# Hymba decoder layer on one core: x's first half in two DMAs, identity products in TensorE's two opening waits, and VectorE's first copy of x placed behind the first unit's low parts

## The chip, the cores and the metric

The kernel runs on one NeuronCore of a Trainium2 chip. The metric is the device time of one execution in microseconds (us), lower is better. The kernel before takes 471.38 us, the median of three runs (470.81, 471.38 and 471.77). TensorE (PE) multiplies, VectorE (DVE) and ScalarE (ACT) work on elements, GpSimd (POOL) builds constants, and SyncE (SP) issues nearly all DMAs from one instruction stream.

## The reference

One decoder layer over 256 tokens of width 1024, all in float32:

```
u = rms_norm(h, norm_mix);  z = u @ w_in
y_rwkv = rwkv7_time_mix(z[..., :RWKV_IN], ...)       # 8 heads of 64
y_moba = moba_attention(q, k, v)                     # 8 heads of 64, from z
h = h + concat[y_rwkv, y_moba] @ w_mix_out
h = h + cross_attention(rms_norm(h, norm_xattn), rms_norm(mem, norm_mem), w_xq, w_xkv, w_xo)
h = h + square(relu(rms_norm(h, norm_ffn) @ w_ff1)) @ w_ff2
out = rms_norm(h, norm_final)
```

The change touches only the beginning: x is read and transposed, and the first column block of `w_in` is multiplied.

## The kernel before

**Tiling.** Every weight matrix is read in units of 1 MB (mostly 1024 rows by 256 columns), three of which fit into the ring `raw`. A float32 product is made from two float32r parts: ACT rounds a half unit into `w_hi` (`hi`, line 1114, `hi_done`), DVE subtracts it from the raw values and gets `w_lo` (`lo`, line 1622, `lo_done`), and PE adds three products (high by high, high weight by low operand, low weight by high operand). The operand x is treated in the same way: PE transposes it in quarters of 256 columns into the banks B[0] to B[3] (`load`, line 616), ACT writes `op_hi` times the norm's gain (line 1166), DVE writes `op_lo` (line 1740), and `copies` (line 1748) keeps the transposed x in `hT` for the residual.

**Order.** There is no scheduler: each engine's order is a list of calls written by hand at the end of its function. PE's starts with `params(0)`, four `load(0, q)`, `dense(2)`, `params(1)`, `dense(2)`, `spread(0)`, and then `dense(10)`. `dense(n)` runs the next n quarters of the weight stream. The first four quarters are unit 0 (lines 515, 516 and 521, halves s=0 and s=1), and `spread(0)` (line 627) spreads the inverse norm. The quarter behind it is the first of unit 1 (line 549), which waits for `hi(2)` and `lo(2)`. A float32 product of 128x128 shows as two records of PE, a transpose or a float32r product as one.

**Waits.** PE's `load(0, 0)` and `load(0, 1)` wait for `x_in[0]`, `load(0, 2)` and `load(0, 3)` for `x_in[1]`. ACT's `stats(0)` (line 1179) takes the row sums of x and needs all of it. DVE's `diagonal_of(0)` (line 1754) waits for their root, and `spread(0)` waits for that diagonal.

**DMA issues.** SP issues in this order: `norm_mix`, first half of x, first half of unit 0, second half of x, second half of unit 0, twelve small parameter rows (line 351), then unit 1 (line 343), two LoRA matrices (lines 353 and 354), unit 2 and `mem`. From unit 3 on it waits for `hi_done` and `lo_done` of the unit that held the buffer; unit 3 needs `lo(1)`.

## Time and profile before

| | before |
|---|---|
| median of 3 runs | 471.38 us (470.81 to 471.77) |
| the profiled execution | 470.57 us, span 468.8 us |
| PE busy | 453.8 us (97%) |
| PE weight loads | 410.1 us (87%) |
| DVE busy | 322.0 us (69%) |
| ACT busy | 236.6 us (50%) |
| DMA queue q1 | 72.14 MB, 48.3% of 16 engines |
| mean DMA rate | 156 GB/s |

The span runs from the first to the last instruction of the profile; the profiled execution's own time is 1.77 us more. PE is busy in 97% of the span, so what matters is the few places where it isn't. "Idle before" in a row is the time in which that engine stood still before the instruction, and the name behind the arrow is what ended it.

### The profile page before, as it was taken

What the parts mean: (1) busy time and instruction counts of PE and PEld (TensorE: products, weight loads), DVE (VectorE), ACT (ScalarE), POOL (GpSimd) and SP (SyncE); (2) the same over time, 40 slices, a digit from 0 to 9 for tenths busy, and PEclk for the clock granted to TensorE, in tenths of its full rate; (3) what the DMA queues carried; (4) which work ended last, traced back from release to release, by engine and by line L of the source; (5) the groups of instructions that cost most, each with busy time, mean ns of one, the idle gap of its engine ahead of it and who ended that gap; (6) DMA issues with size and microseconds to landing.
All of it is one profiled execution on the core that took longest, in us unless ns stands there. A gap on an engine that the chain in (4) does not pass through costs nothing.

```text
span 468.8 us, 10481 instructions
## 1 busy us (share of the span) xinstructions
PE 453.8 (97%) x4470; PEld 410.1 (87%) x4470; DVE 322.0 (69%) x487; ACT 236.6 (50%) x373; POOL 35.1 (7%) x51
## 2 busy tenths in 40 slices
PE   4999999989999999999999999999999999999994
PEld 4999999989899879999998898888888888888883
DVE  4688999897485557668766368876555656574746
ACT  5789833252444426436444455545465545454534
POOL 8200000000000000071000001340000000000000
PEclk9999999999999999999999999999999999999998
DMA  7973534606050432462552165655546565756502
GB/s 246 334 226 119 180 95 142 215 5 184 3 194 15 153 119 89 137 225 89 180 181 89 35 189 189 218 181 179 180 147 213 185 197 166 251 185 218 188 2 89
DMA packets 60385, 73.05 MB, mean 156 GB/s; under 512 B 1314, under 2 KB 49524, under 8 KB 60340
## 3 DMA queue, kind: packets, MB, share of 16 engines
q1 hardware_dynamic: 60260, 72.14, 48.3%
q8 instruction: 35, 0.57, 0.5%
q0 software_dynamic: 80, 0.26, 0.1%
q14 instruction: 10, 0.08, 0.0%
HBM read 71.35 MB, written 1.05 MB: 154 GB/s over the span
## 4 chain that ended last, share of the span: by engine, by line
PE 90%; DVE 4%; DMA 1%; SPq 1%; ACT 1%; issue 1%; ACTq 0%; DVEq 0%
PE bank L534 13%; PE bank L549 11%; PE bank L550 10%; PE bank L551 10%; PE bank L566 6%; PE bank L568 6%; PE bank L567 6%; PE bank L536 6%; PE bank L915 2%; DMA raw<-in_w_in 1%; PE bank L502 1%; PE bank L503 1%; PE bank L504 1%; PE bank L939 1%; PE bank L488 1%
## 5 line engine op out<-in xcount | busy, mean ns | idle before, releaser
L1622 DVE TENSOR_TENSOR w_lo<-raw,w_hi 128x1024 fp32r<-128x1024 f32 x130 | 160.2, 1239 | 67.2 <-ACT w_hi L1114 67.1
L1114 ACT ACTIVATE w_hi<-raw 128x1024 fp32r<-128x1024 f32 x130 | 136.8, 1057 | 111.0 <-PE bank L551 51.8
L534 PE MATMUL bank<-op,w_hi 128*128 128x512 f32 x256 | 89.1, 398 | 0.0
L549 PE MATMUL bank<-op,w_hi 128*128 128x256 f32 x288 | 83.7, 291 | 0.2 <-DVE w_lo L1622 0.2
L550 PE MATMUL bank<-op,w_hi 128*128 128x256 f32 x288 | 81.4, 283 | 0.0
L551 PE MATMUL bank<-op,w_lo 128*128 128x256 f32 x288 | 81.4, 283 | 0.0
L536 PE MATMUL bank<-op,w_lo 128*128 128x256 f32 x224 | 62.8, 281 | 0.0
L549 PEld LDWEIGHTS bank<-op,w_hi 128*128 128x128 f32 x288 | 55.1, 191 | 1.3 <-issue 0.9
L550 PEld LDWEIGHTS bank<-op,w_hi 128*128 128x128 f32 x288 | 55.2, 192 | 0.2
L551 PEld LDWEIGHTS bank<-op,w_lo 128*128 128x128 f32 x288 | 55.1, 191 | 0.0
L534 PEld LDWEIGHTS bank<-op,w_hi 128*128 128x128 f32 x256 | 46.4, 188 | 8.9
L566 PE MATMUL bank<-w_hi,op_hi 128*128 128x512 f32 x128 | 50.0, 390 | 0.0
L568 PE MATMUL bank<-w_hi,op_lo 128*128 128x512 f32 x128 | 49.8, 389 | 0.0
L567 PE MATMUL bank<-w_lo,op_hi 128*128 128x512 f32 x128 | 49.8, 389 | 0.0
L536 PEld LDWEIGHTS bank<-op,w_lo 128*128 128x128 f32 x224 | 42.3, 189 | 1.3
L549 PE MATMUL bank<-op_hi,w_hi 128*128 128x256 f32 x128 | 37.9, 296 | 0.7 <-DVE op_lo L2019 0.7
L550 PE MATMUL bank<-op_lo,w_hi 128*128 128x256 f32 x128 | 36.2, 283 | 0.0
L551 PE MATMUL bank<-op_hi,w_lo 128*128 128x256 f32 x128 | 36.1, 282 | 0.0
L1147 ACT ACTIVATE tmp<-bank 128x256 f32<-128x256 f32 x32 | 12.2, 382 | 37.7 <-PE bank L534 37.6
L568 PEld LDWEIGHTS bank<-w_hi,op_lo 128*128 128x128 f32 x128 | 24.0, 188 | 5.1
L567 PEld LDWEIGHTS bank<-w_lo,op_hi 128*128 128x128 f32 x128 | 24.0, 188 | 5.0
L566 PEld LDWEIGHTS bank<-w_hi,op_hi 128*128 128x128 f32 x128 | 24.0, 188 | 4.7
(275 smaller groups left out, 712.6 us busy)
## 6 DMA issues: line engine op xcount, KB each, us to landing
raw<-in_w_ff SPq DMA_DIRECT2D x32, 1024.0 KB, 5.4
raw<-in_w_in SPq DMA_DIRECT2D x12, 1024.0 KB, 5.5
raw<-in_w_xkv SPq DMA_DIRECT2D x8, 1024.0 KB, 5.3
raw<-in_w_mix_out SPq DMA_DIRECT2D x4, 1024.0 KB, 5.0
raw<-in_w_xq SPq DMA_DIRECT2D x4, 1024.0 KB, 5.0
raw<-in_w_xo SPq DMA_DIRECT2D x4, 1024.0 KB, 5.7
xval<-in_x SPq DMA_DIRECT2D x2, 512.0 KB, 4.7
raw<-in_w_in SPq DMA_DIRECT2D x2, 512.0 KB, 5.7
```

Of the source, the lines that this page charges most:

```text
L534: last = mm(b[:, :], wh[:, k, :], op_both[0][:, :, k, :], start=first, stop=final)
L536: mm(b[:, 0:T], wl[:, k, :], op_hi[0][:, k, :], start=False, stop=False)
L549: mm(dst, wh[:, k, :], op_hi[which][:, k, :], start=first, stop=False)
L550: mm(dst, wh[:, k, :], op_lo[which][:, k, :], start=False, stop=False)
L551: last = mm(dst, wl[:, k, :], op_hi[which][:, k, :], start=False, stop=final)
L566: mm(dst[:, :], hi, wh[:, k, :], start=first, stop=False)
L567: mm(dst[:, :], hi, wl[:, k, :], start=False, stop=False)
L568: last = mm(dst[:, :], lo, wh[:, k, :], start=False, stop=final)
L915: last = mm(dst, xqT[:, 2 * h + a, tokens_of(n)], xkey[:, 2 * h + a, :], start=(a == 0), stop=(a == 1))
L1114: op(view(w_hi), r, ACT.Copy).then_inc(hi_done, 1)
L1147: op(tmp[:, n % 2, T * half:T * half + T], half_bank(s)[:, T:2 * T], ACT.Copy).then_inc(act_part, 1)
L1622: tt(view(w_lo), r, view(w_hi).bitcast(f32), ALU.subtract).then_inc(lo_done, 1)
```

## The change

The first half of x (columns 0 to 511) is read by two DMAs of 256 columns with a semaphore each, so there are three semaphores: PE's `load(0, q)` waits for `x_in[min(q, 2)]`, and ACT's `stats(0)` waits for all three. PE gets `rouse(3)` ahead of `load(0, 0)` and `rouse(5)` between `load(0, 1)` and `load(0, 2)`: float32 products of the identity by itself into a bank that `dense` overwrites later. On DVE `copies(0)` goes from its place behind `load(0, 0)` to behind `lo(1)`.

```
-        x_in, mem_in, mix_in = [sem("x_in0"), sem("x_in1")], sem("mem_in"), sem("mix_in")
+        x_in, mem_in, mix_in = [sem(f"x_in{i}") for i in range(3)], sem("mem_in"), sem("mix_in")
...
             for half in range(2):
-                c, k = slice(512 * half, 512 * half + 512), slice(4 * half, 4 * half + 4)
-                sp.dma_start(stage[0][:, :, c], x[:, :, c]).then_inc(x_in[half], 16)
+                k = slice(4 * half, 4 * half + 4)
+                pieces = (slice(512, 1024),) if half else (slice(0, 256), slice(256, 512))
+                for i, c in enumerate(pieces):
+                    sp.dma_start(stage[0][:, :, c], x[:, :, c]).then_inc(x_in[2 * half + i], 16)
                 sp.dma_start(first_to[:, k, :], first[:, k, UNITS[0][3]:UNITS[0][3] + 256]).then_inc(first_in[half], 16)
...
                 if m == 0:
-                    pe.wait_ge(x_in[q // 2], 16)
+                    pe.wait_ge(x_in[min(q, 2)], 16)
...
+            def rouse(n):
+
+                for _ in range(n):
+                    mm(dense_bank[1][:, 0:128], ident[:, :], ident[:, :], start=True, stop=True)
...
             params(0)
+            rouse(3)
             load(0, 0)
             load(0, 1)
+            rouse(5)
             load(0, 2)
             load(0, 3)
...
                 if m == 0:
-                    act.wait_ge(x_in[0], 16)
-                    act.wait_ge(x_in[1], 16)
+                    for landed in x_in:
+                        act.wait_ge(landed, 16)
...
             params(0)
             load(0, 0)
-            copies(0)
             load(0, 1)
             lo(0)
             load(0, 2)
             load(0, 3)
             lo(1)
+            copies(0)
             diagonal_of(0)
```

This is how TensorE's list begins before the change; L616 is a transpose of x, `x_in0` and `x_in1` are its halves, and L515 is the first product of unit 0.

```order
L595 MATMUL bank<-ident,prob 128x8 [waits mix_in,pool_const]
L616 MATMUL bank<-ident,xval 128x128 [waits x_in0]
L616 MATMUL bank<-ident,xval 128x128 x3
L616 MATMUL bank<-ident,xval 128x128 [waits x_in0]
L616 MATMUL bank<-ident,xval 128x128 x3
L616 MATMUL bank<-ident,xval 128x128 [waits x_in1]
L616 MATMUL bank<-ident,xval 128x128 x3
L616 MATMUL bank<-ident,xval 128x128 [waits x_in1]
L616 MATMUL bank<-ident,xval 128x128 x3
L515 MATMUL bank<-op,w_hi 128x256 [waits dve_op,hi_done]
```

The same stretch of TensorE after the change, where L618 is the transpose, L625 the identity product and L517 the first product of unit 0.

```order
L597 MATMUL bank<-ident,prob 128x8 [waits mix_in,pool_const]
L625 MATMUL bank<-ident 128x128 x3
L618 MATMUL bank<-ident,xval 128x128 [waits x_in0]
L618 MATMUL bank<-ident,xval 128x128 x3
L618 MATMUL bank<-ident,xval 128x128 [waits x_in1]
L618 MATMUL bank<-ident,xval 128x128 x3
L625 MATMUL bank<-ident 128x128 x5
L618 MATMUL bank<-ident,xval 128x128 [waits x_in2]
L618 MATMUL bank<-ident,xval 128x128 x3
L618 MATMUL bank<-ident,xval 128x128 [waits x_in2]
L618 MATMUL bank<-ident,xval 128x128 x3
L517 MATMUL bank<-op,w_hi 128x256 [waits dve_op,hi_done]
```

Three products stand ahead of the first transpose and five ahead of the ninth; nothing else on TensorE has moved.

This is how VectorE's list begins before the change; L1740 writes `op_lo`, L1748 is the copy of x, L1622 writes `w_lo`, and L1754 waits for the root of the row sums.

```order
L1740 SCALAR_TENSOR_TENSOR op<-bank,par,op 128x256 [waits act_op,dve_params]
L1740 SCALAR_TENSOR_TENSOR op<-bank,par,op 128x256
L1748 COPY hT<-bank 128x512 [waits act_op] x2
L1740 SCALAR_TENSOR_TENSOR op<-bank,par,op 128x256 [waits act_op,dve_params]
L1740 SCALAR_TENSOR_TENSOR op<-bank,par,op 128x256
L1622 TENSOR_TENSOR w_lo<-raw,w_hi 128x1024 [waits hi_done]
L1740 SCALAR_TENSOR_TENSOR op<-bank,par,op 128x256 [waits act_op,dve_params]
L1740 SCALAR_TENSOR_TENSOR op<-bank,par,op 128x256
L1740 SCALAR_TENSOR_TENSOR op<-bank,par,op 128x256 [waits act_op,dve_params]
L1740 SCALAR_TENSOR_TENSOR op<-bank,par,op 128x256
L1622 TENSOR_TENSOR w_lo<-raw,w_hi 128x1024 [waits hi_done]
L1754 RECIPROCAL row_sum<-row_sum 128x2 [waits act_root]
```

The same stretch of VectorE after the change, with L1749 for `op_lo`, L1757 for the copy, L1631 for `w_lo` and L1763 for the reciprocal.

```order
L1749 SCALAR_TENSOR_TENSOR op<-bank,par,op 128x256 [waits act_op,dve_params]
L1749 SCALAR_TENSOR_TENSOR op<-bank,par,op 128x256
L1749 SCALAR_TENSOR_TENSOR op<-bank,par,op 128x256 [waits act_op,dve_params]
L1749 SCALAR_TENSOR_TENSOR op<-bank,par,op 128x256
L1631 TENSOR_TENSOR w_lo<-raw,w_hi 128x1024 [waits hi_done]
L1749 SCALAR_TENSOR_TENSOR op<-bank,par,op 128x256 [waits act_op,dve_params]
L1749 SCALAR_TENSOR_TENSOR op<-bank,par,op 128x256
L1749 SCALAR_TENSOR_TENSOR op<-bank,par,op 128x256 [waits act_op,dve_params]
L1749 SCALAR_TENSOR_TENSOR op<-bank,par,op 128x256
L1631 TENSOR_TENSOR w_lo<-raw,w_hi 128x1024 [waits hi_done]
L1757 COPY hT<-bank 128x512 [waits act_op] x2
L1763 RECIPROCAL row_sum<-row_sum 128x2 [waits act_root]
```

The two copies now stand between the second `w_lo` and the reciprocal.

## Rows read from the trace of the kernel before

**Rows 1.** The page: busy time, and the engines of the chain that ended last.

```profile
PE 453.8 (97%) x4470; PEld 410.1 (87%) x4470; DVE 322.0 (69%) x487; ACT 236.6 (50%) x373; POOL 35.1 (7%) x51
PE 90%; DVE 4%; DMA 1%; SPq 1%; ACT 1%; issue 1%; ACTq 0%; DVEq 0%
```

**Rows 2.** PE's waits: engine, line, releaser, us in total, times, longest.

```profile
PE bank L616 <- DMA xval<-in_x: 3.6, 2, 2.0
```

**Rows 3.** The chain that ended last, opening: start us, us, what.

```profile
7.84 6.93 DMA raw<-in_w_in
14.80 1.07 ACT w_hi L1114
15.96 1.24 DVE w_lo L1622
```

**Rows 4.** Timeline of PE: start us, us, instruction, idle before and what ended it.

```profile
4.62 1.97 PE L616 MATMUL bank<-ident,xval 128*128 128x128 f32 x8 [1.96 <-DMA xval<-in_x]
8.28 1.97 PE L616 MATMUL bank<-ident,xval 128*128 128x128 f32 x8 [1.69 <-DMA xval<-in_x]
10.26 0.41 PE L516 MATMUL bank<-op,w_hi 128*128 128x256 f32 x1
10.48 0.41 PE L515 MATMUL bank<-op,w_hi 128*128 128x256 f32 x1
...
12.12 0.28 PE L515 MATMUL bank<-op,w_hi 128*128 128x256 f32 x1
12.24 0.28 PE L516 MATMUL bank<-op,w_hi 128*128 128x256 f32 x1
...
16.54 0.61 PE L627 MATMUL bank<-prob,ones 128*128 128x128 f32 x4
17.33 0.36 PE L549 MATMUL bank<-op,w_hi 128*128 128x256 f32 x1 [0.18 <-DVE w_lo L1622]
```

**Rows 5.** Timeline of SP's issues of x's second half and of unit 1.

```profile
2.22 0.51 SPq L332 DMA_DIRECT2D xval<-in_x  x1
...
7.84 0.39 SPq L343 DMA_DIRECT2D raw<-in_w_in  x1
```

**Rows 6.** Landing, issues at 1.26 and 2.77: KB, us.

```profile
xval<-in_x SPq DMA_DIRECT2D x1, 512.0 KB, 3.3
...
raw<-in_w_in SPq DMA_DIRECT2D x1, 512.0 KB, 6.9
```

**Rows 7.** Stretches: us, busy us of PE to POOL, granted clock, DMA share, GB/s.

```profile
2.30:4.60 2.30, 0.24 (x1) 0.18 (x1) 0.17 (x1) 0.00 (x0) 2.10 (x7) 1.00 0.94 305
...
9.80:11.30 1.50, 1.50 (x9) 1.50 (x8) 1.50 (x3) 1.49 (x5) 1.42 (x2) 1.00 1.07 332
...
460.00:468.80 8.80, 2.85 (x13) 2.03 (x11) 4.34 (x10) 3.60 (x10) 0.00 (x0) 0.81 0.32 119
```

**Rows 8.** Timeline of DVE and ACT in the opening.

```profile
7.51 1.28 DVE L1748 COPY hT<-bank 128x512 f32<-128x512 f32 x2
...
9.44 1.69 ACT L1166 ACTIVATE op<-bank,par 128x256 fp32r<-128x256 f32 x4 [1.03 <-PE bank L616]
...
11.02 1.06 ACT L1114 ACTIVATE w_hi<-raw 128x1024 fp32r<-128x1024 f32 x1
...
12.19 1.29 DVE L1622 TENSOR_TENSOR w_lo<-raw,w_hi 128x1024 fp32r<-128x1024 f32 x1
...
14.65 0.17 DVE L1754 RECIPROCAL row_sum<-row_sum 128x2 f32<-128x2 f32 x1 [1.17 <-ACT row_sum L1185]
```

**Rows 9.** Timeline of PE behind its longest later idle time.

```profile
100.99 1.37 PE L751 MATMUL bank<-neu,X 32*32 32x32 f32 x128 [1.08 <-DVE neu L1889]
...
102.74 0.28 PE L502 MATMUL bank<-w_hi,op 128*128 128x256 f32 x1
```

**Rows 10.** Short stretches: us, granted clock, DMA share, GB/s.

```profile
8.50:9.00 0.50, 1.00 0.51 172
9.00:9.50 0.50, 1.00 1.03 172
```

More of the change, by code:

```diff
@@ L215, in build @@
         raw_in, first_in = [sem(f"raw_in{i}") for i in range(NRAW)], [sem(f"first_in{i}") for i in range(2)]
-        x_in, mem_in, mix_in = [sem("x_in0"), sem("x_in1")], sem("mem_in"), sem("mix_in")
+        x_in, mem_in, mix_in = [sem(f"x_in{i}") for i in range(3)], sem("mem_in"), sem("mix_in")
         act_sums, act_root, dve_diag, pe_spread_rms = sem("act_sums"), sem("act_root"), sem("dve_diag"), sem("pe_spread_rms")
@@ L330, in _ @@
             for half in range(2):
-                c, k = slice(512 * half, 512 * half + 512), slice(4 * half, 4 * half + 4)
-                sp.dma_start(stage[0][:, :, c], x[:, :, c]).then_inc(x_in[half], 16)
+                k = slice(4 * half, 4 * half + 4)
+                pieces = (slice(512, 1024),) if half else (slice(0, 256), slice(256, 512))
+                for i, c in enumerate(pieces):
+                    sp.dma_start(stage[0][:, :, c], x[:, :, c]).then_inc(x_in[2 * half + i], 16)
                 sp.dma_start(first_to[:, k, :], first[:, k, UNITS[0][3]:UNITS[0][3] + 256]).then_inc(first_in[half], 16)
@@ L603, in load @@
                 if m == 0:
-                    pe.wait_ge(x_in[q // 2], 16)
+                    pe.wait_ge(x_in[min(q, 2)], 16)
                 elif q == 0:
@@ L618, in load, with rouse @@
                 last.then_inc(pe_load, 1)
+            def rouse(n):
+                for _ in range(n):
+                    mm(dense_bank[1][:, 0:128], ident[:, :], ident[:, :], start=True, stop=True)
             def spread(m):
@@ L943, in _ @@
             params(0)
+            rouse(3)
             load(0, 0)
             load(0, 1)
+            rouse(5)
             load(0, 2)
@@ L1172, in stats @@
                 if m == 0:
-                    act.wait_ge(x_in[0], 16)
-                    act.wait_ge(x_in[1], 16)
+                    for landed in x_in:
+                        act.wait_ge(landed, 16)
                 else:
@@ L2046, in _ @@
             load(0, 0)
-            copies(0)
             load(0, 1)
@@ L2052, in _ @@
             lo(1)
+            copies(0)
             diagonal_of(0)
```

## The prediction, made before the changed kernel was run

> **What bounds the kernel now.** I read the page's busy times first: PE is busy in 97% of the span and carries 90% of the chain that ended last [rows 1]. So a saving counts only where PE stands still or runs slowly, and whatever delays PE's stream is carried to the end. Next I read PE's waits. The longest are two for x, 3.6 us together [rows 2], both in the opening. Then the chain in order of time shows what holds the end, and it isn't x. The chain goes from the issue of unit 1 at 7.84 through its landing 6.93 us later (14.77) to ACT's rounding at 14.80 and DVE's low part at 15.96 [rows 3], and from there to PE's first product of unit 1 at 17.33 [rows 4]. Last comes PE's own timeline [rows 4]: eight transposes at 4.62, 1.69 us of idle, eight at 8.28, then the 48 products of unit 0 without a gap, the two norm products (four records from 16.54, done at 17.15), 0.18 us of idle, and unit 1. So two paths meet at 17.33: the weights' path ends there, and PE's own path ends 0.18 us before. From 17.33 on I treat the program as one block whose length doesn't change, since PE is full.
>
> The clock matters in that stretch. Products of 256 columns start 0.22 us apart at 10.26, and 0.12 us apart at 12.12 [rows 4]: 256 columns are 0.213 us at 1.2 GHz and 0.107 us at 2.4 GHz, so the lower level holds until about 11.3 and the upper one follows. The granted clock of 9.80 to 11.30 reads 1.00 all the same [rows 7]; in the opening that column says nothing, and I go by the distances. Ahead of the rise PE did eight transposes, idled 1.69 us, and did eight transposes and seven products.
>
> **The change part by part.** The sum is made against the profiled execution, 470.57 us, which lies 0.8 us under the median of 471.38.
>
> *x's first half in two DMAs, on PE's side.* The first half lands 3.3 us after its issue at 1.26 [rows 6], so at 4.56. A quarter is 256 KB less; at 305 GB/s [rows 7] that is 0.86 us, so I expect it at 3.7 to 3.9. The second quarter ends with the same bytes as before, at 4.6 to 5.0. Transposes, ACT's `op_hi` and DVE's `op_lo` of the first quarter start 0.6 us earlier at most.
>
> *The products by the identity.* The two norm products made four records in 0.61 us [rows 4], 0.11 to 0.12 us of distance, so a float32 product is two records. At the lower clock a record of 128 columns takes about 0.21 us, which the transposes show (eight in 1.97 us less the pipeline's 0.2 [rows 4]). `rouse(3)` is then 6 x 0.21 = 1.3 us from 2.45, over by 3.9: it fits in the 1.96 us of idle ahead of the first transpose, or costs 0.2 us there. `rouse(5)` is 10 x 0.21 = 2.1 us against 1.69 us of idle, but starts up to 0.6 us sooner, at 5.6 to 6.0, and is over by 7.7 to 8.1, ahead of x's second half at 8.2. Cost 0, at worst 0.3 us, and PE's path can bear that, as shown next.
>
> *What the clock gives back.* If the upper level is reached by 8.3, eight transposes go from 1.7 to 1.0 us and the seven slow products from 0.21 to 0.12 us each (0.7 us). PE's path gets 1.3 us shorter: its work ends near 15.8 and not at 17.15. It isn't held up earlier: ACT's four `op_hi` at 9.44 [rows 8] and then `w_hi` of s=1 at 11.02 move 0.5 us forward with the transposes, and PE needs the latter at about 12.2.
>
> *`copies(0)` behind `lo(1)`.* Two copies, 1.28 us in all at 7.51 [rows 8]. Where they stood they held up `op_lo` of the second quarter and `lo(0)`. Where they go, DVE has 1.17 us of idle ahead of the reciprocal at 14.65, for it waits for ACT's root. `lo(1)` ends at 13.48 at the latest (12.19 + 1.29 [rows 8]); with the copies DVE is there at 14.76, 0.11 us late in the worst case, and in the likely one `lo(1)` is over by 13.0 and nothing is late. Behind it stand the diagonal, four short parameter operations and `lo(2)`, which has 0.20 us of slack. Cost 0, at most 0.1 us.
>
> *The same split, on SP's side.* SP issues one DMA more ahead of unit 1. Rows of such issues last 0.39 and 0.51 us [rows 5]; I take 0.45, so unit 1 is issued at 8.3 and not at 7.84. Does it land later? Between 8.5 and 9.0 the DMA engines are busy in a 0.51 share, and from 9.0 on in 1.03 [rows 10]. So they ran partly dry before unit 1 came, and there a later issue is a later landing. But the second half of unit 0, issued at 2.77, landed only 6.9 us later, at 9.67 [rows 6], so some engines were still at it in that hole, and on those a later issue costs nothing. The bounds are 0 and 0.45 us; I take 0.35, nearer to the hole's side. It lies in the path of rows 3 and is carried in full.
>
> The Trainium skill says in DMA: Bandwidth & Descriptors (Queues, rings and completion order) that each DMA engine takes descriptors in the order of its ring. By that rule alone, with rings never empty, the later issue would cost nothing and the sum would be 470.6; the half-empty window of rows 10 says that some rings were empty, and the measurement decides for a cost.
>
> *The sum.* PE's path is ready at about 15.8, the weights' path at 17.33 + 0.35 = 17.7. PE's gain of 1.3 us turns into a longer wait for `lo(2)`, about 1.9 us where it was 0.18. 470.57 + 0.35 = 470.9 against the profiled execution.
>
> *The measured median.* The other three runs of the kernel before are 0.24, 0.81 and 1.20 us above the profiled one. One cause that the rows allow: the rise of the clock comes at another moment in each. Every microsecond by which it comes later than 11.3 costs PE's path 0.5 us, and only 0.18 us of it is covered. A rise at 13.5 would be 1.1 - 0.18 = 0.9 us. After the change PE's path has 1.9 us to spare, so that cost is gone. The skill's page TensorE: Matmul & The Clock Gate (Part 1) also says that the number of slow matmuls at the start differs from run to run of one kernel; one trace can't show it. I allow 0.1 us for scatter with other causes and predict 471.0 us, 0.08% under the median.
>
> **The rivals.**
>
> *A. The clock is worth something and unit 1 isn't late.* For it: the slowest DMA engine had no hole, and 1 us of scatter waits to be removed. Against it: rows 10. Then the runs gather at the profiled 470.57 or a bit under: 470.57 less the 0.18 us that PE had to spare and some tenths if unit 1's bytes come sooner, 470.1 to 470.6, say 470.4, 0.2% faster.
>
> *B. The weights' path gets longer by more than the issue.* `lo(1)` ends up to 0.6 us sooner, so SP asks for unit 3 sooner, while unit 1 is still under way on busy engines; and x's first half now comes in rows of 1 KB where they were 2 KB. Each could cost unit 1 a few tenths. For it: the share is over 1.0 from 9.0 on [rows 10]. Against it: `w_in`'s rows are 1 KB too, and the rate with them is 332 GB/s in 9.80 to 11.30, no less than x's 305 [rows 7]. 470.57 + 0.45 + 0.6 = 471.6, no change that can be told.
>
> *C. The clock falls back in the longer wait.* This is the one on the slower side. PE now idles near 1.9 us ahead of unit 1. If that throws it to 1.2 GHz, the products of unit 1 start 0.21 us apart for as long as the rise takes again: from the first product at 9.9 it took 1.4 us, from 8.28 3.0 us, so half of 1.4 to 3.0 us is lost, 0.7 to 1.5, in the one block that carries everything to the end. With the later issue that is 471.6 to 472.4, and it counts as slower once the fall costs over 1.4 us. For it: at the end of the span, where PE has finished, the granted clock is 0.81 [rows 7]. Against it: after 1.08 us of idle at 100.99 the products start 0.12 us apart [rows 9], and the unit 0 work would come right ahead of this wait.
>
> *D. The change doesn't wake the clock.* Products by an identity may not count, or the rise comes at 11.3 anyway. Then PE's path is 0.5 us better at most from x's first quarter, still ahead of the weights' path, and the time is again 470.9. It has the forecast's time, and I count it there.
>
> The skill's page on the clock gate (Part 4, PE-mode transpose) says that transposes don't count as work for the clock; the trace agrees in so far as eight of them at 4.62 were followed by eight more at the lower level. If the page is right, only `rouse` and unit 0 count.
>
> **How the numbers follow.** The forecast (with D) has 0.60, with its own range 470.6 to 471.4. A has 0.20, B 0.11, C 0.09. A difference under 0.2% (0.94 us) can't be told from none here, so faster means under 470.44 and slower over 472.32. A lies on that edge: half of it counts as faster, and I add 0.10 for medians of the forecast's kind that scatter downwards, since the baseline's own median may be high by chance. That is 0.20 faster. C gives 0.05 and scatter 0.03 slower, 0.08. The rest is 0.72. The range takes A's better end and most of C's: 470.1 to 472.0.
>
> **What would show it right or wrong.** Right: first transpose at 3.7 to 4.1; records of the identity products at 2.45 and 5.6; the first product of unit 0 at 9.2 to 9.9, and 0.12 us between products from there; the copies at 13 to 14.4; unit 1 issued at 8.3 and landed at 14.8 to 15.3; PE idle for 1 to 2 us ahead of line 549's first product, which starts at 17.4 to 17.9. It would be wrong if that first product came before 17.2 (then something I take as fixed has moved), if products behind it started 0.21 us apart (C), or if it came at its old place and the time changed by over 1 us, for then my block from there to the end isn't rigid.

## The result and the profile after

The changed kernel takes 473.62 us, the median of 6 runs (472.41 to 474.04). The kernel before, run beside it, takes 471.43 us (6 runs, 470.81 to 471.79). The ratio is 1.0046 with a 95% interval of 1.0036 to 1.0056. The change makes the kernel 2.2 us slower, and the forecast of 471.0 us and its range both missed. The profiled execution after took 474.0 us with a span of 472.0 us, 3.4 us above the profiled execution before (470.57 us).

The page of the kernel after: busy time, and the chain that ended last by engine (before: [rows 1]).

```profile
PE 457.8 (97%) x4486; PEld 413.7 (88%) x4486; DVE 322.3 (68%) x487; ACT 236.5 (50%) x373; POOL 35.4 (7%) x51
PE 89%; DVE 4%; SPq 2%; DMA 2%; ACT 1%; issue 1%; ACTq 0%; DVEq 0%
```

PE is busy 4.0 us longer. The rows of the 16 new records (eight float32 products) sum to 3.96 us (1.65 + 2.31, below) and stand where PE idled before, so the busy time says little of the end. The DMA's and SP's shares of the chain have gone from 1% to 2% each, and this is the first pointer to the opening.

PE's waits after: engine, line, releaser, us in total, times, longest (before: [rows 2]).

```profile
...
PE bank L551 <- DVE w_lo L1631: 1.6, 1, 1.6
PE bank L618 <- DMA xval<-in_x: 1.4, 2, 0.8
PE bank L553 <- issue: 0.9, 1, 0.9
```

The waits for x have gone from 3.6 to 1.4 us, and the wait for unit 1's low part has gone from 0.18 to 1.55 us. That exchange was forecast. The wait of 1.08 us at line 751 [rows 9] is gone, and 0.94 us with no releaser stands near 95 us instead.

PE's timeline after: start us, us, instruction, idle before and its releaser (before: [rows 4]; 618 is before's 616, 625 the identity product, 551 to 553 are before's 549 to 551).

```profile
2.64 1.65 PE L625 MATMUL bank<-ident 128*128 128x128 f32 x6
4.16 1.11 PE L618 MATMUL bank<-ident,xval 128*128 128x128 f32 x4
5.95 1.12 PE L618 MATMUL bank<-ident,xval 128*128 128x128 f32 x4 [0.67 <-DMA xval<-in_x]
6.86 2.31 PE L625 MATMUL bank<-ident 128*128 128x128 f32 x10
9.93 1.10 PE L618 MATMUL bank<-ident,xval 128*128 128x128 f32 x8 [0.76 <-DMA xval<-in_x]
...
10.99 0.28 PE L518 MATMUL bank<-op,w_hi 128*128 128x256 f32 x1
...
16.98 0.68 PE L634 MATMUL bank<-prob,ones 128*128 128x128 f32 x4
19.21 0.52 PE L551 MATMUL bank<-op,w_hi 128*128 128x256 f32 x1 [1.55 <-DVE w_lo L1631]
19.53 0.41 PE L552 MATMUL bank<-op,w_hi 128*128 128x256 f32 x1
19.74 0.41 PE L553 MATMUL bank<-op,w_lo 128*128 128x256 f32 x1
...
22.52 0.36 PE L551 MATMUL bank<-op,w_hi 128*128 128x256 f32 x1
22.71 0.28 PE L552 MATMUL bank<-op,w_hi 128*128 128x256 f32 x1
...
96.02 0.27 PE L553 MATMUL bank<-op,w_lo 128*128 128x256 f32 x1 [0.94 <-issue]
```

Three things are to be seen. The first transpose starts at 4.16 and not at 4.62, but x's second half lets PE go on only at 9.93, where it was 8.28. Unit 0 runs with 0.12 us between products from 10.99 on, its second product, so the clock is up earlier, as hoped. And unit 1 begins at 19.21, 1.88 us later than at 17.33, with products 0.21 us apart until 22.52.

The granted clock after, in short stretches: us, busy us of PE to POOL, clock, DMA share, GB/s.

```profile
18.50:19.00 0.50, 0.00 (x0) 0.00 (x0) 0.50 (x2) 0.18 (x1) 0.00 (x0) 1.00 1.14 391
19.00:19.50 0.50, 0.29 (x1) 0.32 (x2) 0.50 (x2) 0.00 (x0) 0.00 (x0) 0.75 1.03 397
20.00:21.00 1.00, 1.00 (x6) 1.00 (x6) 0.54 (x2) 0.32 (x1) 0.00 (x0) 0.50 1.00 399
...
23.00:24.00 1.00, 1.00 (x10) 1.00 (x10) 0.67 (x3) 0.08 (x1) 0.00 (x0) 1.00 1.10 349
```

The clock falls to its lower level (0.50, 1.2 GHz) just as the wait ends. The 15 products from 19.21 to 22.52 take 3.31 us; at 0.12 us each they would take 1.8. So the fall costs about 1.5 us.

SP's timeline after: start us, us, issue (before: [rows 5]).

```profile
1.27 0.92 SPq L334 DMA_DIRECT2D xval<-in_x  x2
2.23 0.47 SPq L335 DMA_DIRECT2D raw<-in_w_in  x1
2.74 0.51 SPq L334 DMA_DIRECT2D xval<-in_x  x1
3.29 0.47 SPq L335 DMA_DIRECT2D raw<-in_w_in  x1
3.81 1.00 SPq L353 DMA_DIRECT2D prob<-in_norm_mem  x1
4.84 0.89 SPq L353 DMA_DIRECT2D prob<-in_norm_xattn  x1
...
9.38 0.39 SPq L345 DMA_DIRECT2D raw<-in_w_in  x1
```

Landing after of x's second half, issued at 2.74: KB, us (before: [rows 6] for its neighbours).

```profile
xval<-in_x SPq DMA_DIRECT2D x1, 512.0 KB, 7.1
```

Unit 1 is issued at 9.38 and not at 7.84. The extra issue accounts for 0.5 us of that; another 1.0 us comes from the issues of the parameter rows, of which the first two take 1.00 and 0.89 us where they took 0.40 and 0.30. x's second half lands at 9.84. Before, PE could start on it at 8.28.

The chain that ended last, in the kernel after: start us, us, what (before: [rows 3]).

```profile
9.38 7.28 DMA raw<-in_w_in
16.68 1.06 ACT w_hi L1123
```

So the 1.88 us are two amounts: unit 1's issue is 1.54 us later, and its landing takes 7.28 us where it took 6.93, 0.35 more. The path is the one of the forecast, from SP's issues over ACT and DVE.

A stretch of the kernel after, all of it with the granted clock, DMA share and GB/s at the end.

```profile
4.00:6.50 2.50, 1.83 (x9) 1.27 (x8) 0.24 (x1) 0.84 (x2) 2.00 (x8) 1.00 0.60 161
```

The same stretch of the kernel before.

```profile
4.00:6.50 2.50, 1.88 (x8) 1.57 (x8) 0.00 (x0) 0.72 (x2) 2.00 (x8) 1.00 0.97 320
```

This is the place that I hadn't looked at. The same bytes are wanted, but from 4.0 to 6.5 us the 16 DMA engines are busy for 0.60 of the time where it was 0.97, and move 161 GB/s where it was 320. That is (320 - 161) x 2.5 us = 0.4 MB that has to come later.

**The ledger.** First product of unit 1: +1.88 us. Products at the lower clock: +1.5 us. Near 95 us, 0.94 + 0.2 us without a releaser, and 1.08 us less at line 751: about 0. Together +3.4 us, against 472.0 - 468.8 = 3.2 us between the two spans and 474.0 - 470.57 = 3.4 us between the two times. That is one pair of executions. The medians differ by 2.2 us, because the profiled execution before lies 0.9 us under its median of 471.43 and the one after 0.4 us over 473.62.

### The profile page after: what moved, and what is told of

Its sections match the earlier page's. It is cut to its first block, busy times and chain, and to the rows that moved or that the text cites. A ratio compares the mean times of both kernels' runs of the same rounds, so it can differ in the third digit from the quotient of the medians.

```text
span 472.0 us, 10514 instructions
## 1 busy us (share of the span) xinstructions
PE 457.8 (97%) x4486; PEld 413.7 (88%) x4486; DVE 322.3 (68%) x487; ACT 236.5 (50%) x373; POOL 35.4 (7%) x51
## 3 DMA queue, kind: packets, MB, share of 16 engines
HBM read 71.35 MB, written 1.05 MB: 153 GB/s over the span
## 4 chain that ended last, share of the span: by engine, by line
PE 89%; DVE 4%; SPq 2%; DMA 2%; ACT 1%; issue 1%; ACTq 0%; DVEq 0%
PE bank L536 13%; PE bank L551 11%; PE bank L552 10%; PE bank L553 10%; PE bank L568 6%; PE bank L570 6%; PE bank L569 6%; PE bank L538 6%; DMA raw<-in_w_in 2%; PE bank L922 2%; PE bank L504 1%; PE bank L505 1%; PE bank L506 1%; PE bank L946 1%; SPq L353 1%; PE bank L490 1%
## 5 line engine op out<-in xcount | busy, mean ns | idle before, releaser
L1631 DVE TENSOR_TENSOR w_lo<-raw,w_hi 128x1024 fp32r<-128x1024 f32 x130 | 160.2, 1239 | 68.7 <-ACT w_hi L1123 68.6
```

The lines of the kernel that those rows point to most:

```text
L1631: tt(view(w_lo), r, view(w_hi).bitcast(f32), ALU.subtract).then_inc(lo_done, 1)
```

## The experiments

Each kernel was timed against the kernel before on the same chip. Ratios have 95% intervals. "Without the split" means that x's first half comes in one DMA, as before. The tables give the start of unit 1's first product from PE's timeline; in the kernel before it is 17.33 us, with a span of 468.8 us. Every such column is one profiled execution of each kernel, the ratios are of all its runs.

### Which of the three parts costs the time

Split alone, in the kernel before:

```
-                sp.dma_start(stage[0][:, :, c], x[:, :, c]).then_inc(x_in[half], 16)
+                for i, c in enumerate(pieces):
+                    sp.dma_start(stage[0][:, :, c], x[:, :, c]).then_inc(x_in[2 * half + i], 16)
```

> The kernel before with x's first half in two DMAs, and nothing else of the change. Theory T (the split delays the whole input stream): unit 1 lands near 16.7 as in the changed kernel (14.77 before), the first product of unit 1 starts near 19.2, the second half of x comes at 9.8. PE's own path isn't shortened and ends late too, so PE idles little ahead of unit 1 and the clock stays up: 470.6 + 1.9 = 472.5. Rival R (the identity products are the cause, through PE's idle time and the clock): unit 1 lands at 14.8 to 15.2 and the time is 470.6 to 471.4.

Identity products alone:

```
+            rouse(3)
             load(0, 0)
             load(0, 1)
+            rouse(5)
```

> The kernel before with the identity products (3 and 5) and nothing else. Theory T: transfers as before (unit 1 lands at 14.8, its first product at 17.3); PE's path is up to 1.3 us shorter and turns into idle ahead of unit 1 of 1.0 to 1.5 us; if that much idle is enough for the clock to fall, 472.2, and if not, 470.6 to 471.0. Rival R: the clock falls here as it did in the changed kernel, lower level for some 3.4 us, +1.65 us, 472.2 to 473.

Copies moved alone:

```
-            copies(0)
...
             lo(1)
+            copies(0)
```

> The kernel before with copies(0) behind lo(1) and nothing else. All theories: the two copies run at about 13.5 to 14.8 in VectorE's idle time ahead of the reciprocal, unit 1's low part starts within 0.1 us of 15.96, and the time is that of the kernel before, 470.6 to 471.2. If the copies matter: the reciprocal starts 0.5 us or more after 14.65 and the time rises by that.

The changed kernel without the split, and the same kernel again in a later series, beside the changed kernel itself:

```
-                pieces = (slice(512, 1024),) if half else (slice(0, 256), slice(256, 512))
+                c, k = slice(512 * half, 512 * half + 512), slice(4 * half, 4 * half + 4)
```

> The changed kernel with x's first half in one DMA again (identity products and the later copies stay). Theory T: all of the 1.9 us by which unit 1 came late goes, and the clock's fall goes or stays with the idle left ahead of unit 1 (about 1.5 us): 470.6 if it stays up, 472.2 if it falls. Rival R: 473 to 473.6, as the changed kernel.

> The kernel of e4 again, on another chip. If the gain is real: ratio 0.9985 to 0.9995, most runs 0.5 us under the kernel before. If it was the chip: 1.000.

> The changed kernel, unchanged, for its ratio on this chip and a second profile. Theory: the input stream's delay is in every run and the clock's fall in most of them, so the runs lie between 472.0 (no fall) and 474, median ratio 1.0046 as before; unit 1's first product at 18.7 to 19.4 again. If the first profile was an odd one: unit 1's first product before 18 and a ratio under 1.003.

| kernel | median us (runs) | ratio to before | unit 1's first product | span |
|---|---|---|---|---|
| split alone | 472.68 (12) | 1.0032 [1.0020, 1.0044] | 19.75 | 471.2 |
| identity products alone | 470.58 (12) | 0.9988 [0.9977, 1.0000] | 17.84 | 469.4 |
| copies alone | 471.08 (11) | 0.9998 [0.9989, 1.0008] | 18.01 | 469.4 |
| changed, no split | 470.30 (12) | 0.9989 [0.9976, 1.0003] | 17.07 | 468.3 |
| the same again | 470.77 (11) | 0.9997 [0.9988, 1.0006] | 17.45 | 469.5 |
| changed, again | 473.25 (11) | 1.0038 [1.0023, 1.0054] | 18.24 | 469.4 |

The loss needs the split: alone it costs 1.5 us by the ratio (0.9 to 2.1), and without it nothing is lost. The copies show no cost. The identity products, alone or with the copies, gain 0.1% at best, and each interval reaches 1.000.

But the split alone doesn't lose its time on the path of the forecast, and there its expectation missed. Unit 1 was expected to land near 16.7; it is issued at 8.29, 0.45 us later, and lands 6.7 us after that, at 15.0, only 0.2 us later than before. The chain that ended last in that kernel doesn't go through it:

```profile
2.73 7.17 DMA xval<-in_x
9.94 1.97 PE bank L618 x8
...
15.75 0.21 PE bank L517
15.97 0.12 PE bank L518
```

PE's timeline shows no wait ahead of unit 1. Its own path is 2.84 us longer (norm products at 19.38, before 16.54): x's second half is 1.66 us late for PE, and the products of unit 0 stay 0.21 us apart until 15.77 where it was 11.33, which is the other 1.2 us. So the split makes two paths late, PE's own by x's second half, and the weights' by SP's issues and unit 1's landing. In the changed kernel the identity products shorten the first, and the second decides. Apart from the kernel before, with 0.18 us, no kernel without identity products shows a wait of PE ahead of unit 1, so their first product tells of PE's own path.

The column of first products explains most spans: in this table and the next there are twelve kernels besides the two of the first pair, all with unit 1's products at the upper clock from the start, and in nine of them the span is longer by as much as the first product is later, within 0.35 us. The other three have 0.4 to 0.8 us more; the one repeated without the split (+0.12 and +0.7) has 2.4 us on PE without a releaser. The profiled execution of the changed kernel again was its fastest run (471.09 us), with unit 1 at 18.24 (18.7 to 19.4 expected) and no fall:

```profile
18.24 0.36 PE L551 MATMUL bank<-op,w_hi 128*128 128x256 f32 x1 [0.82 <-DVE w_lo L1631]
```

There unit 1 is issued even later, at 9.47, but lands 6.2 us after its issue and not 7.3. The runs of the changed kernel lie between 0.5 and 3.7 us over the profiled execution before (471.09 to 474.26 us).

One profile of each kernel has a scatter of its own. Copies alone has its first product at 18.01, 0.68 us late, and a ratio of 0.9998. So a first product 0.7 us later than 17.33 isn't a loss by itself: the profiled execution before was the lowest of its times (470.57 us; its other six runs took 470.81 to 471.79).

### What the split does to the stream

Two pieces with one semaphore, so that PE starts on nothing earlier; then four pieces of 128 columns (rows of 512 bytes):

```
-                sp.dma_start(stage[0][:, :, c], x[:, :, c]).then_inc(x_in[half], 16)
+                for i in range(1 if half else 2):
+                    part = c if half else slice(256 * i, 256 * i + 256)
+                    sp.dma_start(stage[0][:, :, part], x[:, :, part]).then_inc(x_in[half], 16)
```

> The kernel before with x's first half in two DMAs by columns, both on one semaphore, so no transpose starts earlier. If the transfers alone make the loss: x's second half lands at 9.5 to 10, as in e1 (9.90), and the ratio to the kernel before is 1.003, as there. If the early start has a part in it: x's second half at 8.2 to 8.7 and no change.

> As e15 with four DMAs of 128 columns (rows of 512 bytes). If each DMA more in the queue costs its share: x's second half lands at 12 to 13, two more pieces costing about twice what the first did, ratio 1.009 to 1.012. If the delay is that of an issue slot only (0.45 us each): 9.2 to 10.5, ratio 1.004 to 1.006.

Two pieces by token tile, so that rows stay 2 KB:

```
+                pieces = ... ((slice(0, 1), slice(0, 512)), (slice(1, 2), slice(0, 512)))
+                    sp.dma_start(stage[0][:, n, c], x[:, n, c]).then_inc(x_in[2 * half + i], 16)
```

> As e1, but the first half of x is split by token tile and not by columns: again two DMAs of 256 KB, now of 128 rows of 2 KB where e1 has 256 rows of 1 KB; both are waited for before the first transpose. If the number of DMAs is what delays the stream: unit 1 lands near 16.7, as in e1, 472.5. If it is the shorter rows: the second half of x at 8.2 to 8.7, unit 1 at 14.8 to 15.2, 470.6 to 471.2.

The kernel before with one DMA of 4 KB more behind x's first half:

```
+                    sp.dma_start(spare[0:8, :], io["norm_mix"]...).then_inc(spare_in, 16)
```

> The kernel before with one more DMA, a row set of 4 KB, between x's first half and unit 0's first half; nothing waits for it but the end. It takes the issue slot that the split takes (0.45 us) and adds no bytes. If one more DMA in the stream is enough: x's second half lands at 9.5 or later, and the time is 471.9 to 472.7 as in the two split kernels. If only the issue slot counts: all later issues 0.45 us later, x's second half at 8.2 to 8.7, unit 1 at 14.8 to 15.2, 470.6 to 471.2.

The changed kernel with the second piece issued by ScalarE's queue:

```
+            act.dma_start(stage[0][:, :, 256:512], io["x"]...[:, :, 256:512]).then_inc(x_in[1], 16)
```

> The changed kernel with the second piece of x's first half issued by ScalarE on its own queue ahead of its table load, so that SyncE's stream has as many DMAs as before the change. If the delay comes from what stands in SyncE's one queue: DMA engines busy between 4.0 and 6.5, x's second half at 8.2 to 8.7, unit 1 at 14.7 to 15.3, idle ahead of it under 1.2 us, no fall of the clock, 470.0 to 470.8, as without the split. If the pieces themselves (rows of 1 KB, small DMAs) are what is slow: x's second half at 9.5 or later and 472.5 to 473.6.

The changed kernel without the split and with x in a single DMA:

```
+                if half == 0:
+                    sp.dma_start(stage[0][:, :, :], x[:, :, :]).then_inc(x_in[0], 16)
```

> The kernel of e4 (identity products, later copies) with all of x in one DMA, one DMA less than before the change. x lands at about 6.2 as a whole where its second half came at 8.2, unit 0's halves at 7.7 and 9.3, unit 1's issue 0.5 us earlier. If a DMA less speeds the stream as one more slowed it: unit 1 lands at 13.5 to 14.3 and the time is 469.5 to 470.2 (ratio 0.997 to 0.9985). If bytes set it: unit 1 at 14.5, TensorE's path about as before, ratio 0.9985 to 1.000.

| kernel | ratio to before | DMA share, GB/s in 4.0 to 6.5 us | x's second half landed | first product | span |
|---|---|---|---|---|---|
| before | | 0.97, 320 | 8.2 | 17.33 | 468.8 |
| changed | 1.0046 [1.0036, 1.0056] | 0.60, 161 | 9.8 | 19.21 | 472.0 |
| split alone | 1.0032 [1.0020, 1.0044] | 0.76, 242 | 9.9 | 19.75 | 471.2 |
| two, one semaphore | 1.0035 [1.0022, 1.0049] | 0.79, 196 | 9.9 | 19.71 | 472.0 |
| four, one semaphore | 1.0016 [1.0006, 1.0025] | 0.87, 221 | 9.4 | 18.39 | 470.3 |
| two of 2 KB rows | 1.0013 [1.0002, 1.0025] | 0.79, 240 | 10.5 | 19.62 | 471.4 |
| 4 KB DMA more | 1.0024 [1.0015, 1.0033] | 0.99, 335 | 8.9 | 18.07 | 469.5 |
| second piece by ACT | 1.0010 [0.9996, 1.0025] | 0.85, 267 | 8.5 | 18.21 | 469.4 |
| x in one | 1.0027 [1.0017, 1.0036] | 1.02, 399 | 6.4 (all) | 19.05 | 470.4 |

Every kernel with two pieces on SP's queue, those of the later sections too, has a hole in the DMA engines' work (a share of 0.60 to 0.83 in 4.0 to 6.5 us; 0.95 to 1.04 in the seven profiles with x in two halves and nothing added to SP's queue) and lands x's second half 1.1 us or more late, whether or not PE starts early. The changed kernel again has 0.82. So it isn't PE's earlier transposes or the third semaphore. It isn't a fixed cost of each piece either: four pieces delay x's second half less than two, although SP needs 1.95 us for their issues. Their landing fits the second expectation, 9.2 to 10.5, but their ratio lies under both. With one semaphore, PE's own path ends last in both, and with two pieces unit 1 lands at 16.7 all the same. The DMA of 4 KB makes no hole and unit 1 lands at 14.6, no later than before. Its 0.24% go with x's second half, 0.6 us later on PE's own path.

Issued from ACT, the same piece costs x's second half only 0.3 us. But the engines aren't full there either, only at another time. The same stretch, 3.5 to 5.0 us, with the second piece by ACT and in the kernel before:

```profile
3.50:5.00 1.50, 1.50 (x8) 1.48 (x8) 0.17 (x1) 0.00 (x0) 1.22 (x6) 1.00 0.62 197
```

```profile
3.50:5.00 1.50, 0.38 (x2) 0.38 (x3) 0.00 (x0) 0.00 (x0) 1.22 (x6) 1.00 0.99 336
```

So SP's queue isn't what makes the hole by itself; with the piece on ACT it is over by 5.0 us. Unit 1 still lands at 15.7, 0.9 us late (14.7 to 15.3 expected), the wait ahead of it is 1.64 us (under 1.2 expected), and the interval reaches from 0.9996 to 1.0025.

The stretched issues (1.00 and 0.89 us in the changed kernel, 0.95 and 1.15 in it again) are gone there but for one of 0.62 us. That isn't ACT's doing alone: with the split alone the longest of them is 0.61 us, and 0.68 us occurs before. With two pieces on SP's queue unit 1 is issued 0.45 to 1.63 us later than before, where the rows of parameters stand ahead of it. The Trainium skill says in DMA: Bandwidth & Descriptors (Issuing engines are not separate DMA queues) that issuing from several engines saves only the sequencer's time and that all DMAs run on the same engines. Here the second queue took 1.3 us off the landing of x's second half (9.8 to 8.5), of which the issue that SP no longer makes is 0.5 us (2.74 to 2.22). The rest lies in the 7.1 us from issue to landing, which became 6.3. The changed kernel again has 6.9 us, and the wide one further down 6.6, so the surplus of 0.3 to 0.8 us is a reading and not a rule.

x in one DMA has full engines and no hole, unit 1 lands at 14.4, and it is still slower (a ratio under 1.000 was expected). Its chain that ended last shows why:

```profile
1.26 5.14 DMA xval<-in_x
6.44 1.97 PE bank L617 x8
8.41 2.13 PE bank L624 x10
10.54 0.87 PE bank L617 x4
```

All of x is there at 6.4, and the five identity products behind the eighth transpose, meant for a wait that no longer exists, hold up the other eight for 2.1 us. So this kernel tells nothing against x in one DMA. It shows that identity products are free only in a wait; x in one DMA without them wasn't run.

### Where the rest of unit 1's delay comes from

Unit 1's DMA ahead of the parameter rows, in the changed kernel; and the parameter rows issued by ScalarE, without the split:

```
+            load_unit(1)
             for name, (r, c) in ROW.items():
...
-            load_unit(1)
```

> The changed kernel with unit 1's DMA issued ahead of the twelve parameter rows. If the late issue behind the parameter rows (9.38) is what holds unit 1: it is issued at 3.9 and lands at 13.5 to 14.5, the first product of unit 1 starts at 17.5 to 18.2 (ScalarE's statistics of x are then the limit), the idle time ahead of it is under 1 us, the clock stays up, 471.0 to 471.6. If the stream is held by something that the bytes meet anyway (x's second half at 9.9 still), x's second half lands at 9.8 as in the changed kernel; that isn't changed by this edit.

> The kernel of e4 (identity products and later copies, no split) with the twelve parameter rows issued by ScalarE before its first work, so that SyncE issues unit 1 at 3.3 and not at 7.5. If the issue behind the parameter rows is what makes unit 1 late: it lands at 12.5 to 13.5, ScalarE rounds it behind its statistics at 14.2 where it was 14.53, TensorE's path is the limit, and the first product of unit 1 starts at 16.6 to 16.9 (17.07 in e4): 469.8 to 470.1. If ScalarE's twelve issues (3.6 us) hold up its own work: first operand later than 5.9 and the time 470.3 or more.

With unit 1 first the ratio is 1.0057 [1.0044, 1.0070]. Unit 1 is there when ACT asks for it, but the rows of parameters aren't (first product at 17.5 to 18.2 and 471.0 to 471.6 us were expected). From SP's and PE's timelines of that kernel:

```profile
3.79 0.56 SPq L345 DMA_DIRECT2D raw<-in_w_in  x1
4.39 2.79 SPq L354 DMA_DIRECT2D prob<-in_norm_mem  x1
```

```profile
16.61 0.29 PE L601 MATMUL bank<-ident,prob 82*128 82x82 f32 x1 [3.02 <-DMA prob<-in_rwkv_ln_b]
```

SP's next issue takes 2.79 us. It stands behind 3 MB, where the first parameter row before stood behind 2 MB and took 0.40 us. PE then waits 3.02 us for the last parameter row, the clock falls at 18.3, and unit 1 starts at 21.54. The same instruction takes 0.40 us before and with the split alone, 1.00 and 0.95 us in the two profiles of the changed kernel, and 2.79 us here, so its length is not its own work. A queue that takes no more would explain it, but no run measures that by itself, and the split alone has the same 2 MB ahead of it.

With the parameter rows on ACT the ratio is 0.9996 [0.9986, 1.0005], first product at 17.48. SP issues unit 1 at 3.29 already, and it lands at 14.2, but ACT's rounding of it starts only at 14.84, without a wait for the DMA (14.53 without the split). No gain; 469.8 to 470.1 us was expected for a late issue as the cause, and 470.55 was measured.

### The clock

The changed kernel with six identity products more in the wait for unit 1; then the identity products written 512 columns wide; then both:

```
             spread(0)
+            rouse(6)
             dense(10)
```

```
-                for _ in range(n):
-                    mm(dense_bank[1][:, 0:128], ident[:, :], ident[:, :], start=True, stop=True)
+                    m = min(n, 4)
+                    mm(dense_bank[1][:, 0:128 * m]..., ident[:, :], ident[:, :]...to_broadcast([128, m, 128]), ...)
```

> The changed kernel with six more identity products (12 records, 1.4 us at the upper clock) behind the norm product, in the wait ahead of unit 1. It removes TensorE's idle time there and no transfer. If the idle time is what throws the clock down: the granted clock stays 1.00 and products of unit 1 are 0.12 us apart from the start; 1.65 us less than the changed kernel, 472.0 where that has 473.6. If the clock's fall has another cause (a limit by time or power), the lower level shows all the same and the time stays at 473.6.

> The changed kernel with the same columns of identity products in three wide instructions (384, 512 and 128 columns) where it has eight of 128. It costs the same TensorE time and puts fewer instructions ahead of the stream. In the changed kernel TensorE stands 0.9 us with no releaser near 95 us and its wait for VectorE behind it (1.1 us before) is gone. If that gap comes from how many instructions went before: it is gone here and the 1.1 us wait is back, the time the same, 473 to 474. In all theories the wait ahead of unit 1 stays near 1.6 us and the clock falls, so the lower level shows for some 3.4 us from 19.2.

> e11 with the wait ahead of unit 1 filled by identity products of 768 columns in two instructions. If the idle time is what throws the clock down: granted clock 1.00 from 19 to 23, products of unit 1 0.12 us apart, and 1.5 us less than e11: 471.9 to 472.4. With the few instructions the gaps of 2.3 us of the earlier fill don't show. If the gaps come from the fill itself and not from the number of instructions: 475 or more.

> The kernel of e4 (identity products, later copies, x in two halves) with the same columns in three wide products. If the gap near 95 us comes from the number of instructions: it is gone, TensorE's wait of 1.1 us for VectorE at the small products is back, and the time is 0.2 to 0.4 us under e4's; ratio 0.998 to 0.999. If not: the gap of 1.3 us stays.

| kernel | median us (runs) | ratio to before |
|---|---|---|
| six more in the wait | 479.11 (6) | 1.0165 [1.0138, 1.0192] |
| wide | 471.84 (12) | 1.0028 [1.0012, 1.0045] |
| wide, six more | 472.56 (6) | 1.0042 [1.0027, 1.0057] |
| wide, no split | 470.68 (11) | 0.9992 [0.9982, 1.0001] |

Six products more keep the clock up at this place, which is what they were for: 0.19 us after the product in the row comes the next, where it was 0.32 (PE's timeline of that kernel).

```profile
20.60 0.35 PE L551 MATMUL bank<-op,w_hi 128*128 128x256 f32 x1 [1.33 <-DVE w_lo L1632]
```

But the kernel loses 8 us (472.0 us was expected). 3.3 us of that are there at unit 1's first product, which starts at 20.60, because unit 1 lands at 18.1. The wide kernel with six more has the same landing and starts at 20.66. Why both kernels with a filled wait get unit 1 that late, although the fill stands on PE behind `spread(0)`, no run shows. PE's waits and a stretch of the same kernel show where most of the rest is lost:

```profile
PE bank L551 <- issue: 2.3, 1, 2.3
PE bank L803 <- issue: 2.3, 1, 2.3
```

```profile
92.00:100.00 8.00, 5.71 (x64) 5.24 (x64) 7.28 (x26) 0.60 (x1) 0.00 (x0) 0.82 0.62 204
```

PE stands still twice for 2.3 us with nothing that releases it, and the clock falls behind that. The wide form, of which the wide kernel's waits follow, does the same columns of work with three instructions instead of eight, and its profile has the wait at line 751 back and no gap near 95 us:

```profile
PE bank L761 <- DVE neu L1901: 1.1, 1, 1.1
...
PE bank L806 <- issue: 0.6, 1, 0.6
```

The wide kernel without the split agrees: the wait of 1.1 us is back, the largest gap is 0.3 us. Its time of 470.68 us is only 0.1 us under the narrow one of the same series (0.2 to 0.4 expected), as the gap was covered. So these gaps go with the number of instructions that PE has had before, not with their columns. With none added the largest is 0 to 0.6 us and the wait for `neu` stands (seven profiles); with eight narrow ones it is 0.7 to 1.5 us and that wait is gone or 0.3 us (nine profiles); with fourteen it is 2.3 us, twice (one profile). A gap of about 1 us replaces the wait for `neu`, so it costs little; 2.3 us twice can't be covered.

The wide kernel also idled 1.71 us ahead of unit 1 and kept its clock, with the next product 0.19 us later (a fall was expected):

```profile
18.95 0.35 PE L551 MATMUL bank<-op,w_hi 128*128 128x256 f32 x1 [1.71 <-DVE w_lo L1634]
```

So did the kernel with the second piece by ACT (1.64 us) and the one with identity products alone (1.52 us). In the wide kernel with six more, the clock fell elsewhere, behind 1.91 us of waiting for x's second half:

```profile
10.09 1.24 PE L618 MATMUL bank<-ident,xval 128*128 128x128 f32 x8 [1.91 <-DMA xval<-in_x]
...
11.33 0.42 PE L518 MATMUL bank<-op,w_hi 128*128 128x256 f32 x1
```

The length of the idle time by itself doesn't decide the fall. How often it happens can be estimated from each run's mean granted clock: below 0.996 in 8 of 17 runs of the changed kernel (5 of 6 in the first series, 3 of 11 in the second), in none of the 136 runs of the kernel before beside the experiments, and in none of 12 runs each of the split alone and of the identity products alone. In the second series the three runs below it took 474.0 us (median), and the other eight 472.7, still 1.5 us over the kernel before: the clock is not needed for a loss. In the changed kernel without the split it was 1 run of 23 (472.42 us, the others of its series 470.28), with the second piece by ACT 1 of 11, in the wide kernel 2 of 12, in the wide one with six more 3 of 6. In these, and in the second series of the changed kernel, the runs below 0.996 were 1.3 to 3.2 us above the others. The mark isn't sharp: in the first series the one run above it took 473.33 us, and the shortest, 472.41, had 0.994.

The Trainium skill says in TensorE: Matmul & The Clock Gate (HAM oscillation — how this bites in real kernels) that a long idle gap of PE brings the lower clock back, and (Part 1) that the moments at which the chip looks aren't tied to the kernel's start, so that runs of one kernel differ. The second fits: the changed kernel's clock fell in one of its two profiles and, by the mean clock, in about half of its runs. The gap of 1.55 us with which it fell here is shorter than those that the page warns of.

## Why the prediction was wrong

**The step that failed first** is "the same split, on SP's side". The term was 0.35 us with bounds of 0 and 0.45; it measured 1.88 us in the profiled execution (1.54 of issue, 0.35 of landing), and 0.9 us in the changed kernel's fastest run. I priced one more issue and nothing else. The split also leaves the DMA engines partly idle at 4.0 to 6.5 us, and in the changed kernel the next issues are stretched. Rows 10 looked at the hole ahead of unit 1 only; the share at 4.0 to 6.5 us was 0.97, with nothing to spare, and was never weighed. I gave the quarters the bytes' price at 305 GB/s, as if two DMAs of 256 KB flowed like one of 512 KB. PE's first four transposes came at 4.16 (4.22 with the split alone), some 0.4 us earlier than 4.62 and not 0.86, the second four waited for x until 5.95 (4.6 to 5.0 expected), and x's second half, which the forecast left at 8.2, landed at 9.84. That last one is a second miss, on PE's side: with the split alone it is in the chain that ends last. The direction was rival B's, but its price (1.05 us) was too small, and neither of its reasons holds. Unit 3 wasn't asked for earlier: SP issues it at 14.50, before at 13.57, because `lo(1)` ended later and not sooner. Rows of 1 KB are not needed: with 2 KB rows the hole is there (0.79), although the median loses less (0.13% against 0.32%).

**Rival C** came on top. It said 0.7 to 1.5 us in 1.9 us of idle; the fall cost about 1.5 us after 1.55 us of idle, and by the mean clock it happened in about half of the runs. I had given it 0.09, mostly because 1.08 us of idle at 100.99 leaves the clock up. That row was too weak a witness for a wait 0.5 us longer. C and B were also priced as if only one of them could occur. What makes unit 1 late also makes the wait, so they came together. They needn't: without the split one run of 23 has the low mean clock too.

**"From 17.33 on one block"** held in most profiles: nine of twelve spans grew by what the first product was late, within 0.35 us. It has one soft place, the 1.08 us of line 751, which takes in up to 1 us of gap near 95 us. The eight added products bring such a gap, so they were not free either, only covered. The block also isn't rigid against the clock, as C's fall shows.

**Other signs.** Missed: the first transpose at 4.16 (3.7 to 4.1 expected), by little; unit 0's first product at 10.79 (9.2 to 9.9); unit 1 issued at 9.38 (8.3), landed at 16.7 (14.8 to 15.3) and begun at 19.21 (17.4 to 17.9). Right: identity products hidden by the waits for x, products of unit 0 0.12 us apart from 10.99 on. Copies at 14.32, with the reciprocal behind them at 15.73, 0.04 us behind the end of ACT's root at 15.69; alone they show no cost. PE idle 1.55 us ahead of unit 1 (1 to 2 expected). "PE's gain becomes a wait" is shown by the identity products alone: x's waits shrink from 3.6 to 0.4 us, the wait for `w_lo` grows to 1.5 us, and the ratio is 0.9988.

**The scatter of the kernel before** I had put down to the moment at which the clock rises. Copies alone gives one witness: there unit 0's products stay 0.21 us apart until about 13.4, unit 1 begins 0.68 us later, and the time is 0.58 us over the profiled execution before. The sum said 0.9 us for a rise at 13.5. The identity products, which should take that cost away, gained 0.3 us alone and 0.3 to 0.6 us in the versions without the split (470.30 to 470.77 us, against 470.85 to 471.12), with intervals that touch 1.000. That agrees with a small effect and doesn't show one. Unit 1's own landing also moves: 14.5 in the changed kernel without the split, 14.9 in the same again, 15.3 with the identity products alone. No identity product takes that away.

**What stays open.** Why two DMAs of 256 KB leave the engines partly dry where one of 512 KB doesn't, why four do it less than two, why unit 1's landing moves by 1 us between two profiles of the changed kernel, and what decides in which runs the clock falls. What fills PE's gaps near 95 us was not settled: the trace names no releaser. No version beat the kernel before by more than the measurement can tell; the best are those without the split.

## What to carry to other kernels

Before a DMA at the start of a stream is split, look at the share of the DMA engines behind it. Here it was near 1.0, and the price showed in the landing of the transfers behind the pieces. Work out every path that the change lengthens, with all that stands behind the new issue on that queue, and read the chain that ended last of each single-part kernel before it is taken as a witness: two kernels can lose the same time on different paths. Products that fill a wait have to go when the wait goes. If PE gets idle time in place of slow work, count with the clock falling back in some runs, and don't fill the wait with many small instructions without looking at PE's later gaps.

## What the runs showed of the hardware

- Two DMAs of 256 KB in place of one of 512 KB on SP's queue: DMA share of 4.0 to 6.5 us 0.60 to 0.83 instead of 0.97, x's second half 6.6 to 7.9 us from issue to landing instead of 6.0. With the second issued by ACT 6.3 us, and the engines are partly idle earlier (0.62 in 3.5 to 5.0 us).
- The issue of one and the same parameter row on SP's queue takes 0.40 us before and with the split alone, 0.95 and 1.00 us in the changed kernel and 2.79 us with unit 1 ahead of it.
- The clock fell after 1.55 us of idle in one profile and stayed up after 1.52, 1.64 and 1.71 us in three others. Behind the fall 15 products started 0.21 us apart or more.
- In the opening the granted clock reads 1.00 while products of 256 columns start 0.21 us apart (split alone, 12.0 to 15.5 us).
- Eight more small products at the start of PE's list bring one idle time of 0.7 to 1.5 us near 95 us, fourteen bring 2.3 us twice; three wide ones with the same columns bring 0.6 us or less.
